# Gated delta scan: five 128x128 products per step rewritten as 64x64 quadrant products in two half passes

## The reference

```python
t_inv = triangular_solve(eye + m, eye)               # m: strictly lower, k_beta @ k.T * decay
def step(state, inp):
    q_i, k_i, u_i, w_i, g_i, a_i = inp
    v_new = u_i - w_i @ state                        # w = t_inv @ (k_beta * exp(g)), u = t_inv @ (v * beta)
    o = (q_i * exp(g_i)) @ state + a_i @ v_new
    k_dec = k_i * exp(g_last - g_i)
    state = state * exp(g_last) + k_dec.T @ v_new
    return state, o
```

## Time and profile before

| what | value |
|---|---|
| time, median of 3 runs | 3190.91 us (3189.27 to 3197.0) |
| span of the profiled execution | 3193.7 us |
| the scan's 14 full steps (791.26 to 1106.69 us) | 315.43 us |
| its last two steps (1106.69 to 1135.90 us) | 29.21 us |
| TensorE busy, whole span | 94% (weight loads 76%) |
| VectorE, ScalarE, GpSimd busy | 56%, 41%, 17% |
| mean granted TensorE clock | 0.966 of full speed |

### The profile page before, as it was taken

One profiled execution on the slowest core, in us unless ns is written; L12 is line 12 of the kernel. 1 busy time (PEld: TensorE's weight loads), 2 busy tenths in 40 slices (PEclk: granted clock), 3 DMA queues, 4 the chain that ended last, 5 costly groups with the idle time before them and its releaser, 6 DMA issues. The chain is left out here.

```text
span 3193.7 us, 56404 instructions
## 1 busy us (share of the span) xinstructions
PE 2994.3 (94%) x21251; PEld 2424.3 (76%) x21272; DVE 1786.1 (56%) x3260; ACT 1294.1 (41%) x2704; POOL 551.9 (17%) x475
## 2 busy tenths in 40 slices
PE   7998999897999989899689999999999999989898
PEld 6886998775888856578468888878888757768687
DVE  5755443074776746655565785565775455544333
ACT  5222433154565558611433323433323277720132
POOL 0000000062343400032022322342333100000000
PEclk9999999998999989999899999999999989999999
DMA  4222775243454433255633223443223262143543
GB/s 140 79 79 79 249 263 181 69 145 135 171 179 151 142 104 101 79 188 188 215 110 106 80 67 106 142 164 106 70 70 115 96 205 97 35 177 151 205 145 118
DMA packets 287604, 423.38 MB, mean 133 GB/s; under 512 B 41472, under 2 KB 178688, under 8 KB 281600
## 3 DMA queue, kind: packets, MB, share of 16 engines
q1 hardware_dynamic: 238880, 383.87, 35.5%
q10 hardware_dynamic: 48480, 36.18, 3.6%
HBM read 270.56 MB, written 149.42 MB: 132 GB/s over the span
## 5 line engine op out<-in xcount | busy, mean ns | idle before, releaser
L114 PE MATMUL pj_pp<-h_hi,pj_whi 128*128 128x512 f32 x1152 | 450.2, 391 | 3.7 <-POOL h_lo L3086 3.7
L115 PE MATMUL pj_pp<-h_lo,pj_whi 128*128 128x512 f32 x1152 | 449.2, 390 | 0.0
L116 PE MATMUL pj_pp<-h_hi,pj_wlo 128*128 128x512 f32 x1152 | 449.2, 390 | 0.0
L114 PEld LDWEIGHTS pj_pp<-h_hi,pj_whi 128*128 128x128 f32 x1152 | 217.0, 188 | 49.2 <-issue 4.5
L2913 ACT CAST pj_whi<-w_raw 128x512 fp32r<-128x512 f32 x192 | 119.1, 622 | 326.7 <-PE pj_pp L116 318.1
L116 PEld LDWEIGHTS pj_pp<-h_hi,pj_wlo 128*128 128x128 f32 x1152 | 216.9, 188 | 45.2
L115 PEld LDWEIGHTS pj_pp<-h_lo,pj_whi 128*128 128x128 f32 x1152 | 217.0, 188 | 44.7
L2977 DVE TENSOR_TENSOR pj_wlo<-w_raw,pj_whi 128x512 fp32r<-128x512 f32 x192 | 160.0, 834 | 11.9 <-ACT pj_whi L2913 8.9
L114 PE MATMUL np_pp<-h_hi,np_whi 128*128 128x512 f32 x384 | 150.4, 392 | 0.0
L115 PE MATMUL np_pp<-h_lo,np_whi 128*128 128x512 f32 x384 | 149.9, 390 | 0.0
L116 PE MATMUL np_pp<-h_hi,np_wlo 128*128 128x512 f32 x384 | 149.8, 390 | 0.0
(11 more groups left out here) (406 smaller groups left out, 7244.1 us busy)
## 6 DMA issues: line engine op xcount, KB each, us to landing
w_raw<-in_w_second SPq DMA_DIRECT2D x192, 256.0 KB, 2.9
ds_pk<-scratch_pack SPq DMA_DIRECT2D x32, 1280.0 KB, 7.5
scratch_pack<-rp_out SPq DMA_DIRECT2D x32, 512.0 KB, 2.7
scratch_sig_fm<-pj_ob SPq DMA_DIRECT2D x64, 256.0 KB, 2.1
mb_sg<-scratch_sig_fm SPq DMA_DIRECT2D x16, 1024.0 KB, 7.0
rp_fm<-scratch_qkv_fm SPq DMA_DIRECT2D x96, 128.0 KB, 2.8
scratch_qkv_fm<-np_acc SPq DMA_DIRECT2D x11, 1024.0 KB, 4.8
np_acc<-in_x SPq DMA_DIRECT2D x16, 512.0 KB, 4.1
```

The source lines that it names most:

```text
L114: nc.tensor.matmul(out, ah, bh, start=(first and i == 0), stop=False)
L115: nc.tensor.matmul(out, ah, bl, start=False, stop=False)
L116: mm = nc.tensor.matmul(out, al, bh, start=False, stop=(last and i == n - 1))
```

## The change

The five large products are cut into 64x64 quadrants. A product of one head and direction becomes eight matmuls of 64x64 by 64x128: for each half of the contraction (64 rows) and each half of the output rows (64 columns of the array). They are issued in two half passes ("turns"), each for all four heads and both directions: in turn 0 direction 0 uses the upper half of the contraction and direction 1 the lower half, in turn 1 the other way round, so that the two directions use different halves of the array's rows and write different banks. Turn 1 waits for a new semaphore that turn 0 increments. `row` is no longer a transpose but a product with a 64x64 block of the identity, 64 columns at a time, also in two half passes.

The order changes too. On TensorE turn 0 of row stands ahead of ys(0), and each half pass (both directions) stands where one direction's product stood; query_state's second half pass is split (heads 0, 1 after us(1), heads 2, 3 after ys(3)). On VectorE next_state for d=1 moves from the next step's head to before last_level, next_state for d=0 ahead of first_level, and state_term one place earlier for each direction. On ScalarE both lower_beta groups stand after copies(3).

```diff
+            def crossed(turn, i, half, bank, left, right, first, last, done=None, at=range(4)):
+                if turn:
+                    pe.wait_ge(half, i + 1 + START)
+                for h in at:
+                    for d in D:
+                        r = at_half[d ^ turn]
+                        for g in B:
+                            mm = nc.tensor.matmul(ps[d][at_half[g], bank, cols[h]], left(d, h)[r, at_half[g]],
+                                                  right(d, h)[r], start=(first and turn == 0 and h == 0),
+                                                  stop=(last and turn == 1 and h == 3), skip_group_check=True)
+                        if done and turn and h == 3:
+                            mm.then_inc(done[d], 1)
+                if turn == 0:
+                    mm.then_inc(half, 1)
...
-            def row(i, d):
-                pe.wait_ge(early_in[d], 32 * i + 32 + START)
+            def row(i, turn):
+                if turn == 0:
+                    for d in D:
+                        pe.wait_ge(early_in[d], 32 * i + 32 + START)
+                else:
+                    pe.wait_ge(row_half, i + 1 + START)
                 for h in range(4):
-                    mm = nc.tensor.transpose(ps[d][:, 3, cols[h]], ga[d][:, G_CUM, h:h + 1].to_broadcast([P, P]),
-                                             ident[:])
-                mm.then_inc(row_done[d], 1)
+                    for d in D:
+                        r = at_half[d ^ turn]
+                        for g in B:
+                            mm = nc.tensor.matmul(ps[d][at_half[g], 3, h * P + r.start:h * P + r.stop],
+                                                  ga[d][r, G_CUM, h:h + 1].to_broadcast([HP, HP]), ident[r, r],
+                                                  start=True, stop=True)
...
-            def state_keys(i, u, b, d):
-                pe.wait_ge(pack_in[d][b], 16 * u + 16 + START)
-                pe.wait_ge(state_done[d], i + START)
-                for h in range(4):
-                    mm = nc.tensor.matmul(ps[d][:, 2, cols[h]], pk[d][b][:, h // 2, part(d, "k_fm"), cols[h % 2]],
-                                          state[d][:, h, :], start=True, stop=True)
-                mm.then_inc(ks_done[d], 1)
...
+            def state_keys(i, u, b, turn):
+                if turn == 0:
+                    for d in D:
+                        pe.wait_ge(pack_in[d][b], 16 * u + 16 + START)
+                        pe.wait_ge(state_done[d], i + START)
+                crossed(turn, i, ks_half, 2, lambda d, h: pk[d][b][:, h // 2, part(d, "k_fm"), cols[h % 2]],
+                        lambda d, h: state[d][:, h, :], True, True, ks_done)
...
-                ys(0)
                 if more > 1:
                     for d in D:
                         pe.wait_ge(t_copied[d], i + 1 + START)
-                        row(i + 2, d)
+                    row(i + 2, 0)
+                ys(0)
+                if more > 1:
+                    row(i + 2, 1)
+                state_keys(i, j, b, 0)
                 us(0)
-                state_keys(i, j, b, 0)
+                state_keys(i, j, b, 1)
                 ys(1)
-                state_keys(i, j, b, 1)
+                query_state(i, b, 0)
                 us(1)
-                query_state(i, b, 0)
+                query_state(i, b, 1, range(2))
                 ys(2)
-                query_state(i, b, 1)
+                new_values(i, 0)
                 us(2)
-                new_values(i, 0)
+                new_values(i, 1)
                 ys(3)
-                new_values(i, 1)
+                query_state(i, b, 1, range(2, 4))
                 us(3)
                 key_values(i, b, 0)
                 ys(4)
                 key_values(i, b, 1)
                 us(4)
-                query_new(i, b, 0, range(4))
+                query_new(i, b, 0)
                 if more:
                     last_y(i + 1, 1 - b)
-                query_new(i, b, 1, range(2))
+                query_new(i, b, 1)
                 if more:
                     last_x(i + 1)
-                query_new(i, b, 1, range(2, 4))
```

More of the change, by code:

```diff
@@ L979, in delta_scan @@
         stored = c.sems("stored", 2)
+        row_half, ks_half, qs_half, nv_half, kv_half, qn_half = [
+            c.sem(f"{n}_half") for n in ("row", "ks", "qs", "nv", "kv", "qn")]
         block = c.open_block()
@@ L1196, in step @@
                 fills(0)
-                if i > 0:
-                    next_state(i - 1, 1 - b, 1)
                 turns(1)
+                state_term(i, b, 0)
                 fills(1)
-                state_term(i, b, 0)
+                state_term(i, b, 1)
                 turns(2)
                 fills(2)
-                state_term(i, b, 1)
                 if more > 1:
@@ L1212, in step @@
                 fills(4)
+                next_state(i, b, 0)
                 if more > 1:
@@ L1215, in step @@
                     first_turn(i + 2, b, 0)
-                next_state(i, b, 0)
+                next_state(i, b, 1)
                 if more:
@@ L1336, in step @@
                 copies(2)
-                if more > 1:
-                    lower_beta(i + 2, b, 0)
                 for d in D:
@@ L1342, in step @@
                 if more > 1:
-                    lower_beta(i + 2, b, 1)
+                    for d in D:
+                        lower_beta(i + 2, b, d)
                 copies(4)
@@ L1380, in _ @@
         def _(pe):
-            def row(i, d):
-                pe.wait_ge(early_in[d], 32 * i + 32 + START)
-                for h in range(4):
-                    mm = nc.tensor.transpose(ps[d][:, 3, cols[h]], ga[d][:, G_CUM, h:h + 1].to_broadcast([P, P]),
-                                             ident[:])
-                mm.then_inc(row_done[d], 1)
+            def row(i, turn):
[4 more added lines that the diff above has]
+                    pe.wait_ge(row_half, i + 1 + START)
+                for h in range(4):
+                    for d in D:
[4 more added lines that the diff above has]
+                                                  start=True, stop=True)
+                        if turn and h == 3:
+                            mm.then_inc(row_done[d], 1)
+                if turn == 0:
+                    mm.then_inc(row_half, 1)
+            def crossed(turn, i, half, bank, left, right, first, last, done=None, at=range(4)):
[12 more added lines that the diff above has]
+                    mm.then_inc(half, 1)
             def level_y(k, b, n):
@@ new lines, in new_values, with key_values @@
+            def new_values(i, turn):
+                if turn == 0:
+                    for d in D:
+                        pe.wait_ge(uf_copied[d], i + 1 + START)
+                        pe.wait_ge(x_copied[d], i + 1 + START)
+                        pe.wait_ge(vd_done[d], i + 1 + START)
+                crossed(turn, i, nv_half, 2, lambda d, h: uf[d][:, h, :], lambda d, h: vd[d][:, h, :], True, True, vnew_done)
+            def key_values(i, b, turn):
+                if turn == 0:
+                    for d in D:
+                        pe.wait_ge(gated[d], 2 * i + 2 + START)
+                        pe.wait_ge(vnew_copied[d], i + 1 + START)
+                crossed(turn, i, kv_half, 2, lambda d, h: kdec[d][b][:, h, :], lambda d, h: vnew[d][:, h, :], True, True, kv_done)
@@ new lines, in query_state, with query_new @@
+            def query_state(i, b, turn, at=range(4)):
+                if turn == 0:
+                    for d in D:
+                        pe.wait_ge(gated[d], 2 * i + 2 + START)
+                        pe.wait_ge(o_copied[d], i + START)
+                crossed(turn, i, qs_half, 1, lambda d, h: qg[d][b][:, h, :], lambda d, h: state[d][:, h, :], True, False,
+                        at=at)
+            def query_new(i, b, turn):
+                if turn == 0:
+                    for d in D:
+                        pe.wait_ge(a_ready[d], i + 1 + START)
+                        pe.wait_ge(vnew_copied[d], i + 1 + START)
+                crossed(turn, i, qn_half, 1, lambda d, h: a_t[d][b][:, h, :], lambda d, h: vnew[d][:, h, :], False, True, o_done)
@@ L1533, in _ @@
             pe.wait_ge(ident_in, 16 + START)
-            for d in D:
-                row(0, d)
+            row(0, 0)
+            row(0, 1)
             keep_warm(nc, spare[0], warm, 22)
@@ L1544, in _ @@
                         pe.wait_ge(erow_done[d], 1 + START)
-                        row(1, d)
+                    row(1, 0)
+                    row(1, 1)
                 else:
```

7 lines of the change are left out of this document (removed).

## The result

The changed kernel takes 3292.85 us (3287.81 to 3296.54, 4 runs) against 3192.16: ratio 1.0315, interval 1.0297 to 1.0334, about 100 us slower. The forecast was 3303. The profiled execution has a span of 3290.6, 97 us more than before; 88 us of that are the 14 full steps and 8 the last two.

What follows compares the result with a forecast made beforehand. Delivery of TensorE's instructions was to bound the scan: 6.06 packets x 4.5 = 27.3 us a step, plus 2.5 for load_pack and 0.2 for the clock, 30.0 against 22.53; in all +112, median 3303 us, range 3195 to 3375.

Steps and rivals of the forecast that it cites:

- The mechanism: TensorE in the scan: 752 pairs a step need 6.06 instruction packets, fetched one at a time, so delivery sets the pace.
- The spacing: TensorE's instruction queue: packets 4.5 us apart with nothing else in the way, bounds 3.7 and 5.0; 27.3 us a step.
- The late packet: Scan step: the instruction packet that meets load_pack on the DMA queues comes late, adding 2.5 us a step.
- The clock: TensorE's granted clock in the scan: 0.2 us a step; if it stayed low, 3345 to 3390 us, chance 0.06.
- The sum as a maximum: Scan step: delivery's 27.3 us exceeds TensorE's 15.5 and VectorE's 21.1, so delivery alone was taken as the base.
- The order on VectorE: VectorE's chain in a scan step under the new order: 21.1 us, whatever TensorE does.
- TensorE's work: TensorE's own work in a scan step: 15.5 us with half passes of 0.88, 24.3 at the other bound.
- The drain: TensorE: going between array shapes costs 0.2 us, ten times a step and for row.
- The half-pass waits: TensorE between the two turns of a product: costed at nothing, some 0.2 us each without cover.
- row's loads: load_early, issued 1.28 us later while row moves 0.6 earlier: costed at nothing; if late, row's wait would hold ys(0).
- rival 1: Scan: delivery keeps up, packets under 3.5 us apart, VectorE's 21.1 us a step decides, 3171 or 3188 us; chance 0.13.
- Rival 2: Scan: TensorE's saving comes through because VectorE's waits shrink, 17.7 us a step, 3123 us; chance 0.05.

Runs made afterwards that it cites:

- the flood: Kernel before the change, with 512 small quadrant products (1024 pairs, operands at hand, no loads) added behind the scan's last step: 3213.34 us, ratio 1.0085.
- e7: Changed kernel, with load_pack bringing only 32 of 1280 columns from the third tile on: 3237.42 us, ratio 1.0146 to the kernel before.
- e5: Changed kernel, with half passes in 64x128 tiles, all 128 output rows in one matmul, 592 pairs a step: 3281.10 us, ratio 1.0276.
- e6: Changed kernel, with row as a transpose again, 696 pairs a step: 3283.66 us, ratio 1.0285 to the kernel before.
- e9: Changed kernel, with the five products reading bfloat16 in one pass, 592 pairs a step: 3251.26 us, ratio 1.0196.
- e2: Changed order on all engines, but the old full-array products and row, against the kernel before: 3208.12 us, ratio 1.0044.
- e3: Changed kernel's products and TensorE order, with the old lists on VectorE and ScalarE: 3283.21 us, ratio 1.0280 to the kernel before.
- e4: Changed kernel, with the second half pass of each of the five products taking 32 of 128 moving columns: 3297.94 us, ratio 1.0327.
- e1: Kernel before, with a one-column product ahead of each quadrant product of a level from the second tile on, 776 pairs a step: 3421.85 us, ratio 1.0711.
- e8: Kernel before, with load_pack in four parts of 640 KB, each issued one level later than the last: 3168.36 us, ratio 0.9927.

## Why the prediction held, and where its sum was off

*The mechanism.* That the count of TensorE's instructions becomes the limit held. 752 pairs a step are there; the gaps are "issue", fall at whole packets, and grow from 21.8 to 95.0 us; the flood shows packets 3.70 us apart with nothing else that could hold TensorE. Those 73 us of further gaps and the waits that follow from them (4.25 us on VectorE in one level) are the greater part of the 97. That one packet at a time is under way fits all of it: in none of the fourteen traces do two packets of the scan begin less than 3.4 us apart, although moving one takes only some 1.2 us in the flood (2.0% of 16 engines' 22.19 us for six). When a packet is asked for, no run shows directly. In the flood one begins to move about 1.1 us after each portion starts, also under the portion that ran at the lower clock.

*The spacing.* The term was mis-sized: 4.5 us a packet was taken, 3.70 is measured without loads, which was the lower bound. A packet carries 256 instructions in the flood, and in the scan some 250 matmuls and loads beside the waits (754 in three in e7); 83 packets begin in the 14 steps, 5.93 a step, so delivery alone takes 5.93 x 3.70 = 21.9 us, not 27.3.

*The late packet.* 2.5 us a step was taken, and 0.2 for the clock. The loads cost 3.9 (e7 against the changed kernel): 2.1 as "issue" and 2.1 as TensorE's longer work at the lower clock. The gap itself, 3.26 and 3.54 in new_values, is 0.80 at the same place in e7, so 2.5 to 2.7 of it is the load's, as taken. The clock was the term that was far too small.

*The sum as a maximum.* The step was taken as the larger of delivery and VectorE's chain. They are in fact nearly equal, 21.9 and 21.1, and add to each other in part: without loads a step takes 24.87. A likely reason, argued and not shown, is that time lost to a packet in one level is not made good in the next, where VectorE is late; in e7 both "issue" (65.2 us) and waits for fills (26.2 us) stand in the same steps. This was missed, as was the clock, and the too large spacing made up for both: 27.3 + 2.5 + 0.2 was forecast, 24.87 + 3.94 measured. So that 30.0 came so near 28.81 is luck, though the direction and the mechanism are not. The same reading fits e5, e6 and e9: less delivery does not bring 4.5 us a packet, since another wait stands right behind.

*The order on VectorE.* Walked through at 21.1 us; e2 shows 21.8 to 22.0 and a cost of 14 us by itself, e3 gives back 10. *TensorE's work* was right for the half pass (0.85 against 0.88). *The drain* of the earlier trace rows fits e5, where the blocks keep their 1.16 us. *The half-pass waits*, costed at nothing, do not appear among what ended TensorE's idle time in the scan. *row's loads* were not late: the wait ahead of ys(0) in the step shown is for ScalarE's uf.

*The clock.* More stretches at the lower level were forecast, at little cost. The mean fell to 0.89, and e7, with the same matmuls at 0.99, puts them at 2.1 us of TensorE's work a step. How much of that the time follows is not settled: the runs that lightened the array's work (e4, e9) also lowered the clock.

*The rivals.* Delivery that keeps up (rival 1) would have given 21 us a step, and was to hold from packets under 3.5 us apart; the flood's 3.70 is against it, though by little, and so are the 24.87 of e7. The flood is also against the Trainium skill's sentence that refilling is hidden (Runtime: NRT & Kernel Launch, "Instruction fetch mechanics"), while its block of 256 instructions agrees to the instruction. Rival 2 never came near.

What stays open: how the 4.5 us a step that the change costs without loads divide between delivery and the new order. Of TensorE's idle time, 54.5 us more is "issue" (65.2 against 10.7) and 22.1 more is waiting for fills (26.2 against 4.1), but the two trade with each other: e3, with the same count, has only 42.1 of "issue" and waits for other things instead. e2 puts the order at some 1.4 us a step in the old products' setting (undisturbed steps of 21.8 against 20.4); with the quadrants it was not measured cleanly.

## What to carry to other kernels

Count instructions, not only array time: where a stretch of TensorE code is made of short matmuls, compare its instructions per microsecond with the rate at which they can arrive, which here was 256 in 3.7 us (69 per us). Where loads held the queues, a packet came up to some 2.7 us later. Gaps marked "issue" inside a block of equal instructions, at equal distances in instructions, are the sign. A kernel near that limit can gain from spreading its loads (0.7% here for a change of a few lines), and can lose from a rewriting that cuts matmuls into smaller ones (3.1% here), even if the array's work falls.

## What was not expected of the hardware

The granted clock fell so far with thinner work that the time did not follow: mean 0.89 after the change, 0.78 with thinner products (e4), 0.60 with one-pass products (e9), 0.69 where one-column products were added (e1), against 0.95 before and 1.00 with the loads spread (e8). It is not the size of the instructions alone: e7 has the same matmuls as the changed kernel and 0.99. The drops looked at in the changed kernel and in e1 stand at gaps in which TensorE waited for instructions: the half pass of 1.95 us follows the gap of 3.26, the product of 2.07 us in e1 the gap of 2.97, as the earlier trace rows follows the gap of 2.05. There a late packet costs twice, once as the gap and once as the slower work behind it.

And the packet spacing in the flood, with no load under way, was steady, 3.5 to 4.0 us from portion to portion, whether TensorE ran at the full clock or the lower one. In e7, where TensorE also waits for VectorE, it was 4.0 in one stretch and is 24.87 / 5.93 = 4.2 on the average.
